# A decoder step with mixture of experts: the refills of the down weights move from SyncE's request queue to ScalarE's

## The reference, cut to what matters

```python
def hier_moe(x, w_rg, b_rg, w_re, b_re, w_gate, w_up, w_down):
    ...
    def expert(acc, xs):
        wg, wu, wd, cw = xs
        h = jax.nn.silu(t @ wg) * (t @ wu)
        return acc + (h * cw[:, None]) @ wd, None

    y, _ = lax.scan(expert, jnp.zeros_like(t), (w_gate, w_up, w_down, combine.T.astype(t.dtype)))
```

## Time and profile before

| | |
|---|---|
| median of 3 runs | 1749.45 us (1748.95 to 1749.95) |
| the profiled execution, its own time | 1742.22 us |
| its span, first to last instruction | 1740.1 us |
| TensorE busy | 1475.5 us, 85% of the span |
| VectorE, ScalarE, GpSimd busy | 622.3, 380.3 and 228.3 us |
| moved by DMA | 328.99 MB, of them 275.43 MB through SP's queue |
| expert weights among them | 2 layers x 32 experts x 3 matrices of 1 MB |

### The profile page before, as it was taken

One profiled execution on the slowest core, in us unless ns is written; L12 is line 12 of the kernel. 1 busy time (PEld: TensorE's weight loads), 2 busy tenths in 40 slices (PEclk: granted clock), 3 DMA queues, 4 the chain that ended last, 5 costly groups with the idle time before them and its releaser, 6 DMA issues. The chain is left out here.

```text
span 1740.1 us, 23066 instructions
## 1 busy us (share of the span) xinstructions
PE 1475.5 (85%) x9105; PEld 1003.4 (58%) x9105; DVE 622.3 (36%) x1409; ACT 380.3 (22%) x993; POOL 228.3 (13%) x224
## 2 busy tenths in 40 slices
PE   6999896899987886999785799999977977998880
PEld 3688665799966445555442567666655454554440
DVE  3455403555456114132111643545523041231114
ACT  2144211344422110111011212224413010111111
POOL 0000003111141000222221100101100001232213
PEclk9999997799977897999998799999978987999995
DMA  9611270000054516899995510403433456999984
GB/s 318 178 73 73 61 164 0 1 1 2 1 191 158 216 75 268 329 384 383 395 401 210 188 69 1 182 1 122 182 134 99 179 229 228 386 390 403 399 315 175
DMA packets 106935, 328.99 MB, mean 189 GB/s; under 512 B 19189, under 2 KB 59997, under 8 KB 81951
## 3 DMA queue, kind: packets, MB, share of 16 engines
q1 hardware_dynamic: 90546, 275.43, 43.1%
q0 software_dynamic: 15040, 47.74, 7.7%
q10 hardware_dynamic: 1248, 4.46, 0.6%
HBM read 301.46 MB, written 41.84 MB: 197 GB/s over the span
## 5 line engine op out<-in xcount | busy, mean ns | idle before, releaser
L1919 PE MATMUL pp<-ring,uT 128*64 128x256 f32 x1728 | 229.3, 408 | 41.5 <-issue 31.5
L1919 PEld LDWEIGHTS pp<-ring,uT 128*64 128x64 f32 x1728 | 123.9, 140 | 138.7 <-issue 73.4
L559 PE MATMUL pp<-uT,ring 128*128 128x272 f32 x576 | 136.7, 396 | 0.9 <-PEq L359 0.9
L559 PEld LDWEIGHTS pp<-uT,ring 128*128 128x128 f32 x576 | 109.1, 192 | 22.7 <-issue 1.0
L1601 PE MATMUL pp<-ring,uT 128*128 128x512 f32 x256 | 114.2, 609 | 4.1 <-PEq L135 4.1
L1940 PE MATMUL pp<-ring,uT 128*64 128x512 f32 x432 | 103.1, 598 | 1.2 <-ACT uT L1970 1.2
L1958 DVE COPY uT<-pp 128x128 f32<-128x128 f32 x64 | 18.7, 292 | 232.8 <-PE pp L1929 232.8
L1964 ACT ACTIVATE uT<-pp 128x128 f32<-128x128 f32 x64 | 17.8, 278 | 379.0 <-PE pp L1919 379.0
L2095 POOL DMA_INDIRECT expert_rows<-uT,row_of_slot x64 | 64.7, 1011 | 244.7 <-ACT uT L1970 244.7
L1601 PEld LDWEIGHTS pp<-ring,uT 128*128 128x128 f32 x256 | 49.9, 196 | 67.5 <-issue 67.5
L1907 PE MATMUL pp<-consts 64*128 64x64 f32 x512 | 70.2, 280 | 18.2 <-DMA consts<-normed_rows,token_of_slot 18.2
(11 more groups left out here) (611 smaller groups left out, 2507.9 us busy)
## 6 DMA issues: line engine op xcount, KB each, us to landing
ring<-in_w_exp_gate SPq DMA_DIRECT2D x54, 1024.0 KB, 21.5
ring<-in_w_exp_up SPq DMA_DIRECT2D x54, 1024.0 KB, 28.1
ring<-in_w_exp_down SPq DMA_DIRECT2D x54, 1024.0 KB, 27.3
ring<-in_w_in_a SPq DMA_DIRECT2D x4, 3072.0 KB, 11.6
scaled_rows<-in_w_exp_gate SPq DMA_DIRECT2D x10, 1024.0 KB, 25.1
scaled_rows<-in_w_exp_up SPq DMA_DIRECT2D x10, 1024.0 KB, 29.4
expert_rows<-zero_rows SPq DMA_DIRECT2D x4, 2048.0 KB
scaled_rows<-in_w_exp_down SPq DMA_DIRECT2D x10, 512.0 KB, 22.3
```

The costliest lines, as they stand in the source:

```text
L559: TE.matmul(pp[n % 2][:, at], w[:, j, ct * P:(ct + 1) * P], uT[:, j, t], start=(j == 0), stop=(j == DJ - 1))
L1919: ins = TE.matmul(pp[0][q * SLOTS:(q + 1) * SLOTS, b * 512:b * 512 + 2 * P], xT[b][:, j, :], w[:, :, j, q, :], start=(j == 0), stop=(j == ...
```

## The change

ScalarE requests the down block of expert e + 5 right behind its copy of the result of expert e - 1, whose down matmuls were the last readers of that slot. It has waited for `s.dn` for that copy anyway, so no wait is added. SP drops `behind` from the loop, with its waits, and goes from one `ahead` to the next. The first six experts' blocks are requested by SP as before, and so are the weights of the code for experts with over 64 rows, which does not run with these inputs.

```diff
@@ -2058,11 +2058,8 @@
                             for k in range(DEEP + 1, DEEP + 1 + STEP):
                                 e = i * STEP + k
                                 ahead(sp, main, e, k % STEP, bass.ds(e, 1))
-                                behind(sp, main, e - 1, (k - 1) % STEP, bass.ds(e - 1, 1))
                         for e in range(DEEP + 1 + loops * STEP, NE):
                             ahead(sp, main, e, e % STEP, slice(e, e + 1))
-                            behind(sp, main, e - 1, (e - 1) % STEP, slice(e - 1, e))
-                        behind(sp, main, NE - 1, (NE - 1) % STEP, slice(NE - 1, NE))
                         if prefetch:
                             prefetch(sp, main)
                         sp.wait_ge(s_d, steps["over"])
@@ -2168,6 +2165,9 @@
                         for e in range(1, NE):
                             silu(act, main, e, e)
                             keep(e - 1)
+                            n = e - 1 + DEEP
+                            if n < NE:
+                                fetch_down(act, main, n % DEEP, slice(n, n + 1))
                         keep(NE - 1)
 
                         n = count(act)
```

## The result

The changed kernel takes 1769.42 us (median of 5 runs, 1764.09 to 1779.62) against 1748.95 us (5 runs, 1744.06 to 1749.95). The ratio is 1.0126, with a 95% interval of 1.0096 to 1.0157: 20.5 us slower, where the forecast was 15.7 us.

A forecast was written before the change was run, and what follows sets the result against it. DMA engines bound the late expert loops, TensorE waiting for gate and up. 4.94 + 2.7 + 4.99 + 3.1 = 15.7 us on the profiled 1742.2 us, plus 7.2 us to the median, gave 1765.2 us; own range 1759 to 1770, wider 1752 to 1776.

The forecast's parts named there:

- The first wait: TensorE's first idle time before L1919 in the changed kernel, expected at expert 12 or 13; before, at expert 17.
- The 46.4 us: TensorE's listed waits in both expert loops before the change, taken as the whole time it stands there.
- the engines stay full either way: Reason why idle times that begin four or five experts sooner are given back before the loop's end.
- First term: Loop end: down blocks of experts 30 and 31 go ahead of the last up block, 4.94 and 4.99 us later.
- Second term: Last three experts: blocks land faster than TensorE's own pace of 6.78 us, losing 2.7 and 3.1 us.
- The bytes are the same: Both loops: only the order in which the DMA engines work moves, not the amount.
- the bound of five experts in the second term: Own-pace loss at the loop's end if it holds for five experts, not three: 4.6 and 5.2 us; total 1769.2 us.
- No change: Rival: down blocks keep their place by age behind what SP handed over; 1749 to 1753 us, chance 0.13.
- Faster: Rival: two queues keep the DMA engines fuller; a 5% rate rise gives 1742.6 us, chance 0.07.
- ScalarE is held: Rival: requests hold ScalarE as they hold SP, up to 7.32 us, 9.5 us more per layer; 1784 us, chance 0.08.
- the 6 us of the earlier trace: Stretch where ScalarE stored rows while SP's weights loaded: both queues moved 2.52 MB, 420 GB/s, without gathers and scatters.

The follow-up runs named there:

- the second trace: The changed kernel profiled and timed once more, nothing altered: 1768.93 us, ratio 1.0110 to the kernel before.
- the one with down two experts ahead: The changed kernel, with ScalarE requesting each down block two experts before its use instead of six: 1760.36 us, ratio 1.0076 to the kernel before.
- the last block in halves: The kernel before, with gate and up of expert 31 requested in column halves so TensorE can start on the first: 1746.22 us, ratio 0.9993.

## Why the prediction was right, and where its sum was short

**Right, with its mechanism.** The first wait was to come at expert 12 or 13 (it came at 13 and 12). The stalls were to end near expert 28 (the last are at 29 and 27, in the second trace at 28 in both layers), the last three experts to run at 6.78 us. Down requests were to cost 0.33 to 0.45 us and land in 7 to 12 us: they cost 0.33 to 0.46 us and land after 11.1 us in the median, but 22 of the 60 take longer than 12 us, up to 16.7. The last up block was to land after all down blocks (958.0 against 942.2 us). The two sides of the order were tried separately: one block ahead of the last up block on SP alone delays it, and two put back behind it give 4.6 to 5.3 us per layer back. Two readings of the prediction were too broad. The 46.4 us were not all of TensorE's idle time in the loops but its waits for weights; another 11.5 us, at the first experts above all, stay without the down refills too. And "the engines stay full either way" ends some 10 us ahead of the last up block, where the share is 0.55 and 0.31.

**First term.** Two blocks ahead of the last up block were to cost 4.94 and 4.99 us. The experiment that puts them back gives 4.6 and 4.8, by the second trace 4.7 and 5.3. That term held. The landing of the last down block was a good measure for it, which fits engines that lag and now have the two blocks to move first.

**Second term.** TensorE's own pace at the end was to cost 2.7 and 3.1 us, for three experts. It measured 2.8 and 5.3 us, in the second trace 2.7 and 2.7. From expert 28 to expert 31 the up blocks land 6.0 and 5.9 us apart, where 5.87 and 5.75 us had been worked out. The 5.3 us hold a stretch at half clock, in layer 1 of the first trace. TensorE's timeline there:

```profile
1696.49 3.68 PE L1919 MATMUL pp<-ring,uT 128*64 128x256 f32 x16 [3.76 <-issue]
```

The table by stretches:

```profile
1695.00:1705.00 10.00, 8.51 (x41) 4.92 (x43) 0.98 (x2) 0.00 (x0) 1.24 (x2) 0.51 1.01 400
```

TensorE had been idle for 3.76 us, the granted clock is 0.51, the lower of its two levels (1.2 of 2.4 GHz), and 16 matmuls last 3.68 us instead of 1.98. From there on no wait could take up the delay, as the blocks were landing ahead of TensorE.

**The step that was mis-sized** is the rate. The prediction said "The bytes are the same" and left the rate of the DMA engines as it was; only a rise stood among the rivals (420 GB/s), with 0.07. It fell, by 0.5 to 1% where the engines are full, worth 1.5 and 2.0 us in the changed kernel. The experiment with the old order at the end and the two queues kept shows the last up block 1.9 and 2.1 us late with the same bytes at the same DMA share, and these are what the sum left out: 4.7 + 5.3 (order), 1.9 + 2.1 (rate) and 2.7 + 2.7 (own pace) make 19.4 us for the second trace, where the loops show 19.1. For the first trace they make 4.6 + 4.8 + 1.9 + 2.1 + 2.8 + 5.3 = 21.5 us, where the loops show 21.2, the half clock in them. These parts are differences of the same landings, so they have to add up; what they show is where the time went. The measured median, 1769.42 us, lies just inside the forecast's own range of 1759 to 1770 us: the mechanism was right, and the range had room for the missing term by the bound of five experts in the second term, which is not where it came from.

Why the rate falls stays open: the two queues could cost it in switching, or the mix with gathers and scatters differs in a slower loop. In that 200 us stretch of layer 0, three kernels with two queues moved 386 to 389 GB/s in four traces (386 is the one with down two experts ahead, whose engines were not full at first), and three with SP's queue alone 390 to 392; in layer 1 it was 386 to 391 against 392 to 395. But the kernel with all refills on ScalarE, again one queue, moved 389 in layer 0 at a share of 1.02. (Its 381 in layer 1 hold a stretch of 20 us at 262 GB/s, out of line with all the rest.) So that the second queue is the cause is not shown.

**The rivals.** "No change" fell with the landings of 11.1 us: a block in the second queue keeps no place by age. The Trainium skill's rule behind it ("DMA: Bandwidth & Descriptors", section "Issuing engines are not separate DMA queues") agrees with the trace on throughput, 388 GB/s against 391 at a share of 1.02. Its reading that only issue time is at stake does not fit: the order of landings alone was worth 9.4 to 10.0 us. "Faster" fell with the rate. "ScalarE is held" was not true of the changed kernel, and true of the one with all blocks on ScalarE, where the bound was too low as well: 11.6 us for the longest request, not 7.32.

## What to carry to other kernels

When the DMA engines are full, do not expect bandwidth from moving requests to a second queue: here it added none (388 GB/s, before 391). It changes which block comes first, since a block in the short queue overtook those in the long one. Ask which block is needed last but is requested early, and what then goes ahead of the one that is awaited; count those blocks at the loop's own rate, and add what the consumer can't make up at the end. Full on average is not full at the end: while the last block was awaited here, half of the engines or more had little left to move. Read a loss from the loop's length, not from the list of waits: here the waits named 10 of 21 us.

## What the runs showed of the hardware beyond expectation

- Two queues with full engines moved a little less than SP's queue alone (387 to 389 against 390 to 392 GB/s in layer 0); the 6 us of the earlier trace rows, at 420, had pointed the other way. ScalarE's queue alone moved 389, so the cause is open.
- In the last 10 us ahead of the landing that ends the weights' loading, the share of busy DMA engines was 0.55 and 0.31: a block of 1 MB was held up by a part of the 16 engines.
- Over the 200 us of the table the mean granted clock fell from 0.99 and 0.97 to 0.95 and 0.92, with waits that were fewer but longer (longest 6.8 us, before 3.6 us). The longest wait does not settle it: with the last block in halves it was 0.95 in layer 0 too, at waits of 3.2 us at most.
- The price of a request went with what its queue held, on either engine: 0.33 us on ScalarE with one or two blocks in it, up to 11.6 us with all of them there; on SP 0.33 us early in the loop and up to 7.7 us late, in the kernel before.
